# The first expert pair's columns made by matrix products instead of a gather, and two column loads requested earlier

## What is computed

```
xp = xp + g1 * mix                                   # mix = heads @ w_o
h  = rms_norm(x, g_ffn) * (1 + sc2) + sh2            # sc2, sh2, g2: rows of 2048, one per group of tokens
g_logits = h @ w_rg + b_rg                           # 4 groups, the best one is taken
e_logits = h @ w_re + b_re                           # 8 experts in each group, the best two are taken
y = sum over the two experts of  w * (silu(h @ w1[e]) * (h @ w3[e])) @ w2[e]
x = x + g2 * y
```

## Time and profile before

| | us |
|---|---|
| median of 3 runs | 1799.03 |
| lowest, highest | 1798.24, 1799.43 |
| the profiled execution's own time | 1802.11 |
| its span, first to last instruction | 1800.3 |
| PE busy in the span | 1636.7 (91%) |
| DVE busy | 630.5 (35%) |
| ACT busy | 268.1 (15%) |
| POOL busy | 103.9 (6%) |

### The profile page before, as it was taken

One profiled execution on the slowest core, in us unless ns is written; L12 is line 12 of the kernel. 1 busy time (PEld: TensorE's weight loads), 2 busy tenths in 40 slices (PEclk: granted clock), 3 DMA queues, 4 the chain that ended last, 5 costly groups with the idle time before them and its releaser, 6 DMA issues.

```text
span 1800.3 us, 18867 instructions
## 1 busy us (share of the span) xinstructions
PE 1636.7 (91%) x6967; PEld 676.1 (38%) x6967; DVE 630.5 (35%) x1369; ACT 268.1 (15%) x713; POOL 103.9 (6%) x193
## 2 busy tenths in 40 slices
PE   4899999999989699977799999999999999999997
PEld 1435545544444344433333233323332333233322
DVE  1212313211326211151344434443444444434445
ACT  1002322111213100000110111011101110111011
POOL 3001200011001100000000000000000000000000
PEclk7899999999999899988899999999999999999998
DMA  9797363566549822077799999999999999999993
GB/s 343 285 342 270 114 245 150 223 251 229 234 167 385 327 94 94 24 280 320 315 415 427 430 427 429 424 428 427 422 427 426 423 428 428 427 426 425 427 428 154
DMA packets 92925, 582.29 MB, mean 323 GB/s; under 512 B 9352, under 2 KB 24552, under 8 KB 55632
## 3 DMA queue, kind: packets, MB, share of 16 engines
q1 hardware_dynamic: 84944, 554.20, 75.8%
q0 software_dynamic: 6208, 22.98, 3.3%
q10 hardware_dynamic: 1728, 4.51, 0.6%
HBM read 586.14 MB, written 7.05 MB: 330 GB/s over the span
## 4 chain that ended last, share of the span: by engine, by line
PE 67%; DMA 17%; issue 2%; DVE 2%; ACT 1%; POOL 0%; SPq 0%; POOLq 0%; ACTq 0%; DVEq 0%
PE bank L1170 23%; DMA ring<-in_w 14%; PE bank L933 13%; PE bank L1029 8%; PE bank L1079 7%; PE bank L1188 3%; PE bank L836 3%; PE bank L1014 2%; PE bank L1123 1%; DMA r<-h_d,gat_now 1%; PE bank L1065 1%; DMA mod_t<-mod_d 1%; PE bank L1003 1%; PE bank L1152 1%; PE bank L995 1%
## 5 line engine op out<-in xcount | busy, mean ns | idle before, releaser
L1170 PE MATMUL bank<-ring,r 128*64 128x512 f32 x1920 | 470.5, 620 | 42.7 <-DMA ring<-in_w 42.7
L1170 PEld LDWEIGHTS bank<-ring,r 128*64 128x64 f32 x1920 | 129.8, 140 | 301.2 <-issue 301.2
L933 PE MATMUL bank<-ring,r 128*128 128x384 f32 (+1 forms) x672 | 241.5, 518 | 0.0
L1798 DVE TENSOR_TENSOR bank<-bank,r 128x512 f32<-128x512 f32 x192 | 134.3, 699 | 264.2 <-PE bank L1079 264.2
L1188 PE MATMUL bank<-ring,mod_row 128*64 128x512 f32 x960 | 209.3, 593 | 8.5 <-ACT mod_row L1370 8.5
L1029 PE MATMUL bank<-ring,r 128*128 128x512 f32 x384 | 169.8, 595 | 0.4 <-issue 0.4
L933 PEld LDWEIGHTS bank<-ring,r 128*128 128x128 f32 x672 | 126.1, 190 | 108.7 <-issue 44.8
L1079 PE MATMUL bank<-r 128*128 128x512 bf16 x576 | 159.5, 388 | 5.5 <-DVE gains L1819 3.0
L1800 DVE TENSOR_TENSOR r<-r,bank 128x512 f32<-128x512 f32 x192 | 131.9, 687 | 6.6
L1188 PEld LDWEIGHTS bank<-ring,mod_row 128*64 128x64 f32 x960 | 80.5, 137 | 126.9 <-issue 116.0
L1079 PEld LDWEIGHTS bank<-r 128*128 128x128 bf16 x576 | 41.7, 98 | 181.2 <-DVE r L1800 102.5
(11 more groups left out here) (261 smaller groups left out, 1173.2 us busy)
## 6 DMA issues: line engine op xcount, KB each, us to landing
ring<-in_w SPq DMA_DIRECT2D x180, 2048.0 KB, 16.9
ring<-in_w_mod SPq DMA_DIRECT2D x96, 1024.0 KB, 11.8
ring<-in_w SPq DMA_DIRECT2D x19, 1024.0 KB, 5.7
ring<-in_w_in SPq DMA_DIRECT2D x24, 768.0 KB, 6.2
ring<-in_w_o SPq DMA_DIRECT2D x16, 1024.0 KB, 10.3
ring<-in_w_in SPq DMA_DIRECT2D x8, 1024.0 KB, 5.3
r<-mod_d POOLq DMA_DIRECT2D x8, 1024.0 KB, 15.4
r<-in_w SPq DMA_DIRECT2D x5, 1024.0 KB, 8.2
```

What stands on the lines that cost most here:

```text
L933: mm = pe.matmul(acc[a % 3][:, 0:w], h_t[:, k, t * P:(t + 1) * P], wu[:, j, :], start=(k == 0), stop=(k == KD - 1))
L1170: mm = pe.matmul(ps[64 * c:64 * c + 64, :], xg_t[:, j, 64 * c:64 * c + 64], big_cut(slot_of(u), (8, 512))[:, j % 8, :], start=(j == 0), st ...
L1798: v.tensor_tensor(y_ps[k % 4][:, :], y_ps[k % 4][:, :], g2b[:, min(t, 1), cols], ALU.mult).then_inc(strip_scaled, 1)
```

## The change

First, the columns `xg_t` of the first expert pair are no longer fetched through DRAM. The 0/1 table says which token is in which slot, so a product of h2 with it gives the wanted columns at once: for each of the 16 column sets j, `xg_t[:, j, :]` is the sum over the three token tiles of h2[:, t, j::16] (stationary) times the table of tile t (moving, 128x128, now float32). That is 48 products of 128x128, in four PSUM banks; ACT and DVE copy these banks to `xg_t`. The products with the token numbers, `gat_now` for the first pair, the first gather and its 16 transposes are gone. The table has one form per tile, made by adding the two ranks (`first_slot`) and one comparison. The last tile's choice now stands before its normalisation on DVE. SP waits for `pick_full` before it loads u14 to u16 over h2. The gather of the second pair stays where it was on POOL's list; only the counts of its waits are changed.

Second, the four transfers for the scale and shift columns are issued in the last attention stage, as soon as the rows are in DRAM, and not behind the six transfers of 1 MB.

```diff
-        first_ps0 = tab_ps[:, 0:2]
+        pick_ps = (bank[2], bank[3], bank[4], bank[6])
...
                     elif u == EXTRA[0] + 2:
                         sp.wait_ge(h2_out, TILES * 16)
+                        sp.wait_ge(pick_full, 4)
...
-            def first_rows_of(t):
+            def pick(t, b):
 
-                pe.wait_ge(first_at, t + 1)
-                for c in (2 * t, 2 * t + 1):
-                    mm = pe.matmul(first_ps0, at_first[:, c, :, :].rearrange("p h s -> p (h s)"), row_b[:, t, :],
-                                   start=False, stop=(c == ASSIGN - 1))
+                for i in range(4):
+                    j = 4 * b + i
+                    mm = pe.matmul(pick_ps[b][:, i * P:(i + 1) * P], h2[:, t, j::KD],
+                                   at_first[:, t, :, :].rearrange("p h s -> p (h s)"),
+                                   start=(t == 0 and i == 0), stop=(t == TILES - 1 and i == 3))
                 return mm
...
-            pe.matmul(first_ps0, ones_b[0:1, :], row_b[0:1, TILES, :], start=True, stop=False)
-            first_rows_of(0)
-            first_rows_of(1)
             logits(last_no)
+            for t in range(TILES - 1):
+                pe.wait_ge(h2_ready, t + 1)
+                pe.wait_ge(first_at, t + 1)
+                for b in range(4):
+                    pick(t, b)
             tile_rank(2, 1).then_inc(rank_full, 1)
-            first_rows_of(2).then_inc(first_row_full, 1)
+            pe.wait_ge(h2_ready, TILES)
+            pe.wait_ge(first_at, TILES)
+            for b in range(4):
+                pick(TILES - 1, b).then_inc(pick_full, 1)
...
             def turn_next(m, backs=True):
 
-                pe.wait_ge(xg_in, m * 16 + 48)
+                pe.wait_ge(xg_in, m * 16 + 32)
+                if not backs:
+                    pe.wait_ge(rank_taken, 1)
...
-            pe.wait_ge(rank_taken, 1)
-            pe.wait_ge(xg_in, 16)
-            turn_x(0)
-            turn_x(1)
...
-            x_out(1, 0)
-            x_out(2, 1)
+            for b in (0, 2):
+                e.wait_ge(pick_full, b + 1)
+                e.activation(xg_t[:, 4 * b:4 * b + 4, :].rearrange("p a b -> p (a b)"), pick_ps[b][:, :],
+                             ACT.Copy).then_inc(xt_read_a, 1)
...
-                v.tensor_tensor(at_first[:, two, :, :],
-                                K("slots").rearrange("p (h s) -> p h s", h=2).unsqueeze(1).to_broadcast([P, 2, 2, CAP]),
-                                own_rank.unsqueeze(3).to_broadcast([P, 2, 2, CAP]), ALU.is_equal).then_inc(first_at, 1)
+                after(v.tensor_tensor(first_slot[:, t, :], first_rank[:, 2 * t, :], first_rank[:, 2 * t + 1, :], ALU.add))
+                v.tensor_tensor(at_first[:, t, :, :], K("slots").rearrange("p (h s) -> p h s", h=2),
+                                first_slot[:, t, :].unsqueeze(2).to_broadcast([P, 2, CAP]), ALU.is_equal).then_inc(first_at, 1)
...
+            choose(2)
             normalised(2)
-            choose(2)
             first_slots(2)
-            v.wait_ge(first_row_full, 1)
-            after(v.tensor_copy(first_token[:, :], first_ps0))
-            v.scalar_tensor_tensor(out=gat_now[:], in0=first_token[:, 0:1], scalar=float(P), in1=first_token[:, 1:2],
-                                   op0=ALU.mult, op1=ALU.add).then_inc(gat_ready, 1)
+            for b in (1, 3):
+                v.wait_ge(pick_full, b + 1)
+                v.tensor_copy(xg_t[:, 4 * b:4 * b + 4, :].rearrange("p a b -> p (a b)"), pick_ps[b][:, :]).then_inc(xt_read_v, 1)
...
+                elif s == ("qk", first_b + 6):
+
+                    g.wait_ge(row_out, 3 * 32)
+                    for x, n in enumerate((SC2, SH2)):
+                        for c in range(2):
+                            g.dma_start(cols_t[:, x, c, :].rearrange("p (cc i) -> p cc i", cc=4),
+                                        mod_d[n, c].rearrange("(cc p i) -> p cc i", cc=4, i=4)).then_inc(cols_in, 16)
...
-            g.wait_ge(h2_out, TILES * 16)
-            g.wait_ge(gat_ready, 1)
-            g.wait_ge(xg_clear, 1)
-            gather()
             g.dma_start(tokens, ins["consts"][:, n_const:n_const + T]).then_inc(tokens_in, 16)
             g.wait_ge(row_out, 4 * 32)
             g.wait_ge(extra_free, 2)
...
-            g.wait_ge(xt_full, 2)
-            g.wait_ge(xg_in, 16)
+            g.wait_ge(h2_out, TILES * 16)
+            g.wait_ge(xg_clear, 1)
             g.wait_ge(tab_ready, 1)
-            g.tensor_copy(gat_now[:], row_tab[:, 1:2]).then_inc(gidx, 16)
-            g.wait_ge(gidx, 16)
+            after(g.tensor_copy(gat_now[:], row_tab[:, 1:2]))
             gather()
```

39 lines of the change are left out of this document (15 added, 24 removed).

## The result

| | median us | lowest, highest |
|---|---|---|
| kernel before, timed beside it | 1799.07 | 1798.24, 1799.43 |
| changed kernel | 1787.53 | 1783.58, 1787.99 |

The ratio is 0.9932, with a 95% interval of 0.9914 to 0.9949: faster by 11.5 us. I had forecast 21.1 us and 1778.0, with a range up to 1783.0. So the sign was right, and the time lies outside the range, 9.5 us above the forecast. The profiled execution took 1787.96 with a span of 1786.1.

The account below looks back on a forecast made before the run. The prediction took the expert loop as bound by its weight stream and the output projection by PE; 14.0 + 7.1 = 21.1 us off the 1799.03 median gave 1777.9, so 1778.0 us, range 1771.5 to 1783.0.

Parts of the forecast that it names:

- The columns, 14.0 us: Start of output projection: early column loads remove PE's 12.43 us wait and speed the shift row's products by 1.6 us.
- Rival (d): Last attention stage: early column loads hold up the weight stream, making the kernel slower, 1818 at 60 us cost; chance 0.03.
- The products, 7.1 us: Behind the projection: products replace first store, gather and transposes on PE's path; second gather lands 7.1 us earlier.
- so I take 0.12: 64 records are 7.7 us: New products on PE: 0.12 us per record, 7.7 us for tiles 0 and 1, 3.85 us for tile 2.
- the 13.5 of the prediction: Behind the projection: w1 products start at 810.7 instead of 824.24, 13.5 us earlier.
- From there to the landing: DMA engines: after h2's store, 17.0 MB stand in one row before the second gather, which lands 7.1 us earlier.
- 858.4: Landing of the second gather on the clock of the kernel before, instead of 865.5.
- 4.4 us for a store of h2: Skill page's figure for the 1.05 MB store; the prediction kept 10.45 us and said 4.4 would improve the sum about 6 us.
- (b): New products: lower clock or costlier strided operand; landing at 861.5, gain 18 us, 1781.5; chance 0.12.
- (a): Second gather lands earlier through a faster store or better share for POOL's transfers; typically 1773.5, at most 1772; chance 0.2.
- (c): One part fails: PE meets another projection wait, or the loop takes nothing over; 1785 to 1792; chance 0.1.

Follow-up runs that it names:

- cols_only: Kernel before with only the four scale and shift column loads moved into the last attention stage; 1785.41 us, ratio 0.9922.
- perm: Changed kernel with h2 stored so the new products' stationary operand has step 1, not 16; gathered rows and transposes follow; 1782.45 us, ratio 0.9895.
- picks_only: Kernel before with only the products in place of the first gather, column loads left late; 1798.59 us, ratio 0.9991.
- cols_early: cols_only with the second pair's gather issued ahead of the two g2 transfers; 1775.24 us, ratio 0.9849.
- stride1: Changed kernel with only the new products' stationary operand read at step 1, so wrong values and only times used; 1783.28 us, ratio 0.9895.

## Why the prediction was wrong

**The columns, 14.0 us: right.** No wait of PE took its place; DVE's residual at 613.13 was done 7 us before it was wanted, the shift row's products took 2.11 us against 2.1. The step from one to the next product block gained 13.3 us in the changed kernel and 14.1 in `cols_only` and `perm` (596.24 to 612.18, 596.94 to 612.89). The 0.8 us between them are the first step's own time, 14.84 us against 13.97: in the changed kernel's profile the clock had fallen ahead of it, in that of `cols_only` not.

```profile
590.00:594.00 4.00, 1.87 (x11) 1.40 (x10) 2.42 (x11) 1.51 (x5) 2.08 (x4) 0.89 1.05 387
594.00:598.00 4.00, 3.15 (x14) 2.45 (x12) 0.53 (x2) 0.49 (x1) 0.00 (x0) 0.50 1.03 411
```
```profile
590.00:594.00 4.00, 1.87 (x14) 1.55 (x14) 2.25 (x11) 1.51 (x5) 1.91 (x4) 1.00 1.04 382
594.00:598.00 4.00, 2.99 (x13) 1.67 (x12) 0.58 (x2) 0.49 (x1) 1.56 (x3) 1.00 1.06 422
```

`picks_only`, whose attention stage is that of the kernel before, shows 0.98 and 0.50 in the same two windows, so the early loads are not its cause. It also differs between executions of the same code: `cols_early` is `cols_only` up to this point, and has 0.55 in 594 to 598 and a first step of 16.40 us. What makes the clock fall in one execution and not in the other stays open. Rival (d) did not happen.

**The products, 7.1 us: wrong, 1.1 measured.** The step that failed is one number: "so I take 0.12: 64 records are 7.7 us". Measured were 14.19 and 7.21 us, 0.22 per record. I had taken 0.12 from six attention products of the same shape, whose stationary operand lies in a row, and had seen in the diff that the new one is `h2[:, t, j::KD]`, with 64 bytes from value to value. The same sum with the new number: 96 records take 21.4 us and not 11.5, so w1 starts 3 us earlier than in `cols_only` and not 13. `perm` and `stride1`, with the operand in a row, have the 7.39 and 3.81 us and w1 at 182.1 and 183.7 us from the second step, against 196.7 before: 13 to 14.6 us earlier, the 13.5 of the prediction.

**From there to the landing: the reasoning held, its input didn't.** I had written that PE could be 4 us slower in its products without moving the landing. It was 10 us slower (21.4 us and not 11.5), and more than PE hangs on it: SP's new wait for `pick_full` stands in front of u14 to u16, a wait that my sum never priced, since by 0.12 per record it was over before the store. With the true pace it ends at 807.7, 5 to 6 us after the store, which was issued at 791.8 and took 10.4 us. The row of bytes then begins at 808. DMA queues of the changed kernel from 808 to 852 (packets, MB, share):

```profile
q1 hardware_dynamic: 1728, 14.68, 80.4%
q0 software_dynamic: 432, 2.54, 13.9%
```

That is 17.2 MB where I had 17.0, at 0.427 MB per us 40.3 us, until 848.3 from 808; the gather landed at 852.2, 44.2 us after 808, where I had 42.3 from the start of the row to the landing. In `perm`, where the store is the gate (landed at 801.4), the gather landed at 844.7, 43.3 us later. My 858.4 on the clock of the kernel before is 844.4 on the later one, 14.0 us earlier. So the size of the row and its starting event were right as soon as the pace was, and its length to 1 to 2 us.

One reading of the prediction was wrong without moving the sum: that the trace "disagrees" with 4.4 us for a store of h2. The 10.45 us are those of the third tile's store, which shares the engines with u12 and u13. The first tile's store, of the same size, had them to itself and landed in 4.2 us. The kernel before, 752 to 760 and 800 to 811 (out<-in, queue, count, KB each, median us to landing; the third of the x3 is issued when the store has landed):

```profile
h_d<-r POOLq DMA_DIRECT2D x1, 1024.0 KB, 4.2
```
```profile
r<-in_w SPq DMA_DIRECT2D x3, 1024.0 KB, 5.5
h_d<-r POOLq DMA_DIRECT2D x1, 1024.0 KB, 10.5
```

Where the store is the gate, its time is thus set in part by the two transfers beside it; what it would bring to hold those back was not tried. (Nor would 4.4 us have made the sum 6 us better, as the prediction says: in it the products end at 810.4, and SP waits for them, so 814.6 - 810.4 = 4.2 us are left.)

**The sum.** With the quick pace of the sum, `perm` is 17.4 us faster in its medians (1799.84 to 1782.45) against 21.1. In the cut profiles it is 14.1 us of the first part and 6.2 us of the second step to w2, 20.3 together. The profiled executions and the medians differ by some 3 us, also for the kernel before, whose profiled execution took 1802.11 and lay 3.1 above its median; my rule to carry that difference over assumed it to be constant, and for the changed kernel it was 0.4. So the forecast of 1778.0 would not have been met even then, and 1782.45 would have lain inside the range but near its end.

**The rivals.** What happened is the second half of (b), "the strided stationary operand costs more than in attention", which had a chance of 0.12. Its path on PE was well priced, for the wrong reason: "the 96 records would cost 22 us ... and the products would start at about 821", and they started at 807.8, which is 820.4 on the clock of the kernel before. Its landing was not: 861.5 let u14 to u16 pass before, as if only u17 waited. Their 3.15 MB stood in the same row. With that it would have been near no gain at all, which `picks_only` shows. (Its 1781.5 is also half a us off its own sum, 1799 - 18 = 1781.) The first half of (b), the lower clock, happened as well, for about the first 6 of the 14 us. Against it I had held that the products follow the projection without a pause; in the changed kernel PE was busy for 1.31 us of the 2 ahead of them (783 to 785, clock 0.81). It cost nothing that shows, because at step 16 the loads took 310 ns at either level. That both halves have about the same price, 22 us for the 96 records, is a coincidence of 333 ns at the lower clock with 310 at the step. (a) did not happen in the changed kernel; the landing was at no time limited by the store's speed. In (c), "one of the two terms goes, and 1785 to 1792 is left", the number fits by luck, since the mechanism was another: nothing kept the loop from taking over what reached it, but only 1.1 us did. (d) is excluded by `cols_only`.

Could the kernel before have told it? It has loads with this step, in the transposes of gathered rows, and groups by line of its loop show them beside those of attention (ns shortest/median/longest):

```profile
L1065 PEld LDWEIGHTS bank<-cst,r x23: 186/196/210, 1039.8 to 1099.9; 128*128 128x128 f32 x23
```
```profile
L1014 PEld LDWEIGHTS bank<-r x16: 186/191/192, 561.2 to 569.3; 128*128 128x128 f32 x16
```

L1065 are the transposes, L1014 is attention. That looks harmless, 196 against 191 ns. Only `perm` shows that a transpose's load with step 1 takes 140 ns (138/140/142, 32 loads of the loop), so that the step costs there too. In the code of before only the transposes (L1065, L1103) have a strided stationary operand of this size, and no row of it had such a product, and for an operation that no row shows the pace needed both ends, 0.12 and 0.23 us, with more than 0.12 of the chance on the upper one.

## What to carry to other kernels

Price a new product by a row with the same steps of its operands and not only the same shape: a float32 stationary operand with fewer than two values in 16 bytes took 310 to 335 ns to load instead of 192, and in a chain of such products, in which the loads are busy all the time, 32 records took 7.21 us instead of 3.81. When an engine's step becomes the release of a buffer, ask what else waits for that buffer: here the slow products cost nothing on PE's own path up to the gather, and what they cost came through SP's wait. And when a transfer stands behind others that wait for something it doesn't need, look at its place first: moving one gather ahead of the two g2 transfers in POOL's list gave 10 to 12 us, while the 48 products gave between nothing (step 16) and 7 us (step 1, h2 stored first). What a part is worth depends on which wait is last, so compare versions that differ in that part alone.

## What the runs showed of the hardware

- The load of a float32 stationary operand of 128 columns: 192 ns at step 1, 197 at 2, 261 at 3, 330 at 4, 318 at 6, 335 at 8, 312 at 16, all at granted clock 1.00. Above 4 it does not rise further. At 0.50 it was 333 ns at step 1 and 310 at step 16: with the large step the clock made no difference.
- A transpose of 128x128 float32 is the same case on a smaller scale: its load took 140 ns at step 1 and 196 at step 16 (`perm` and before, 1000 to 1100).
- A store of 1.05 MB from SBUF to DRAM landed in 4.2 us with the DMA engines to itself and in 10.5 us beside two weight loads of 1 MB.
- DVE's operation of 128x2048 float32 with two inputs took 2.35 us with all operands in a row, 3.79 us with a written step of 512 bytes, 3.84 us with both inputs read in steps of 64 bytes: reading and writing in steps cost nearly the same.
- The stretch ahead of the projection, the same work in every kernel, ended between 594.6 and 601.8 us. In six of the profiles PE's waits for the first weights (in_w_mod) sum to 12.1 to 13.6 us; the granted clock of the first 100 us was 0.81 to 0.93. How the 7 us divide was not worked out. Single executions of one version differ by up to 9.6 us (`perm`), so the median of 4 to 6 can be 2 to 3 us off (an estimate from these ranges), and a stretch of a profile that starts behind that point is the finer measure.
